# Hybrid encoder with PEER experts: one store for two blocks' GELU values, and transfers moved from ScalarE to SyncE

## The reference

```python
q = (xc @ w_q).reshape(c, PEER_HEADS, 2, PEER_HALF_DIM)
sc = jnp.einsum('chpd,hpnd->chpn', q, sub_keys)
top_s, top_i = lax.top_k(sc, kk)                  # 16 of 128 per half
...
cand_s, cand_i = lax.top_k(cand.reshape(c, PEER_HEADS, kk * kk), kk)
experts = i1 * PEER_N_KEYS + i2                   # 16 of 16384 per head
gates = jax.nn.softmax(cand_s, axis=-1)
act = gelu(einsum('chkd,cd->chk', u[experts], xc))
out = einsum('chk,chkd->cd', gates * act, v[experts])
```

## Time and profile before

| | us |
|---|---|
| runs shown (3): median, lowest, highest | 3271.24, 3267.51, 3274.54 |
| the profiled execution: its time, its span | 3269.31, 3267.5 |
| TensorE busy (share of the span) | 3141.4 (96%) |
| VectorE, GpSimd, ScalarE busy | 2429.8, 1987.1, 1451.7 |
| mean granted TensorE clock | 0.987 of 2.4 GHz |
| ScalarE waiting for the `gelu_d` store, both layers | 177.6 in 76 waits |

### The profile page before, as it was taken

One profiled execution on the slowest core, in us unless ns is written; L12 is line 12 of the kernel. 1 busy time (PEld: TensorE's weight loads), 2 busy tenths in 40 slices (PEclk: granted clock), 3 DMA queues, 4 the chain that ended last, 5 costly groups with the idle time before them and its releaser, 6 DMA issues. The chain is left out here.

```text
span 3267.5 us, 61700 instructions
## 1 busy us (share of the span) xinstructions
PE 3141.4 (96%) x18584; PEld 2847.5 (87%) x18584; DVE 2429.8 (74%) x5191; ACT 1451.7 (44%) x2596; POOL 1987.1 (61%) x1588
## 2 busy tenths in 40 slices
PE   8998999999899999999899999999998989999997
PEld 8878889999898888888798787999998988888886
DVE  1475548888776799999915746488887867999998
ACT  2464234444676533333324633444446764333332
POOL 3454348888664566666545543588886645666665
PEclk9999999999999999999999999999999999999999
DMA  4002139999797799999820021499998967999996
GB/s 166 32 2 78 53 111 325 328 325 329 260 349 259 260 336 336 336 334 331 278 90 24 2 85 58 143 321 322 325 307 266 347 246 278 335 335 335 335 331 224
DMA packets 255581, 779.16 MB, mean 238 GB/s; under 512 B 30176, under 2 KB 97504, under 8 KB 247520
## 3 DMA queue, kind: packets, MB, share of 16 engines
q1 hardware_dynamic: 170400, 455.75, 41.9%
q0 software_dynamic: 78336, 285.25, 23.5%
q10 hardware_dynamic: 6720, 36.74, 2.9%
HBM read 692.66 MB, written 83.89 MB: 238 GB/s over the span
## 5 line engine op out<-in xcount | busy, mean ns | idle before, releaser
L723 POOL TENSOR_TENSOR st_lo<-st_raw,st_hi 128x1024 fp32r<-128x1024 f32 x290 | 697.5, 2405 | 416.2 <-ACT st_hi L1003 410.4
L1003 ACT CAST st_hi<-st_raw 128x1024 fp32r<-128x1024 f32 x544 | 569.9, 1048 | 659.1 <-PE ps L2194 615.9
L2091 PE MATMUL ps<-t_hi,st_hi 128*128 128x368 f32 (+1 forms) x2288 | 780.8, 341 | 0.8 <-ACT st_hi L1003 0.7
L2092 PE MATMUL ps<-t_lo,st_hi 128*128 128x368 f32 (+1 forms) x2288 | 770.5, 337 | 0.0
L837 POOL TENSOR_TENSOR wt_lo<-w_f,wt_hi 128x384 fp32r<-128x384 f32 x256 | 416.3, 1626 | 317.6 <-ACT wt_hi L1167 317.5
L2095 PE MATMUL ps<-t_hi,st_lo 128*128 128x368 f32 (+1 forms) x2288 | 448.1, 337 | 3.6 <-POOL st_lo L723 3.5
L2091 PEld LDWEIGHTS ps<-t_hi,st_hi 128*128 128x128 f32 x2288 | 430.3, 188 | 13.3 <-ACT st_hi L1003 3.0
L2092 PEld LDWEIGHTS ps<-t_lo,st_hi 128*128 128x128 f32 x2288 | 430.8, 188 | 10.1
L2095 PEld LDWEIGHTS ps<-t_hi,st_lo 128*128 128x128 f32 x2288 | 394.6, 188 | 17.2 <-POOL st_lo L723 6.2
L2194 PE MATMUL ps<-st_hi,wt_hi 128*128 128x512 f32 x1536 | 390.0, 389 | 2.7 <-ACT wt_hi L1167 2.7
L2194 PE MATMUL ps<-st_lo,wt_hi 128*128 128x512 f32 x1536 | 389.7, 389 | 0.0
(11 more groups left out here) (236 smaller groups left out, 5141.9 us busy)
## 6 DMA issues: line engine op xcount, KB each, us to landing
st_raw<-in_peer_u SPq DMA_DIRECT2D x256, 512.0 KB
st_raw<-in_peer_v SPq DMA_DIRECT2D x256, 512.0 KB
gelu_d<-h_out SPq DMA_DIRECT2D x256, 184.0 KB
h_in<-gelu_d SPq DMA_DIRECT2D x256, 184.0 KB
gates_d<-g_stage ACTq DMA_DIRECT2D x32, 1024.0 KB
g_ch<-gates_d SPq DMA_DIRECT2D x56, 512.0 KB, 6.0
w_raw<-in_w_in SPq DMA_DIRECT2D x16, 1168.0 KB, 5.2
st_raw<-in_peer_w_q SPq DMA_DIRECT2D x32, 512.0 KB
```

The source lines that it names most:

```text
L723: nc.gpsimd.tensor_tensor(st_lo[:, s].rearrange("p c f -> p (c f)"), st_raw[:, r], st_hi[:, s].rearrange("p c f -> p (c f)").bitcast(F32), ...
L1003: nc.scalar.copy(st_hi[:, r % 2].rearrange("p c f -> p (c f)"), st_raw[:, r]).then_inc(st_h, 1)
L2091: nc.tensor.matmul(dst, st_hi[:, s, c], t_hi[:, c, rows], start=c == 0, stop=False)
L2092: nc.tensor.matmul(dst, st_hi[:, s, c], t_lo[:, c, rows], start=False, stop=False)
```

## The change

`h_out` gets four buffers in two pairs, `gelu_d` is laid out by pairs, and a store moves the two blocks of a pair (`gelu_store(i, q)` waits for both GELUs). ScalarE's GELU of a pair waits for the store of the pair two before. The transfers of `idx`, `x_x`, `h_x` and the gate stores are no longer issued by ScalarE; SyncE issues them, between its loads, in an order that is written out from block 88 on. Some small tiles (`idx_x`, `e_x`, `h_x`, `idx_u`, `idx_b`, `dot_8`) move to where `wt_hi` and `wt_lo` of the v half lie. TensorE's, VectorE's and GpSimd's instructions are the same, in the same order.

```diff
-    h_out = pr.tile("h_out", [P, 2, TN], F32)
+    h_out = pr.tile("h_out", [P, 2, 2, TU], F32)
...
-    gelu_d = nc.dram_tensor("gelu_d", [EB, P, TU], F32, kind="Internal").ap()
+    gelu_d = nc.dram_tensor("gelu_d", [EB // 2, P, 2, TU], F32, kind="Internal").ap()
...
-            def gelu_store(i, s):
+            def gelu_store(i, q):
-                sp.wait_ge(gelu_done, EB * l + 2 * i + s + 1 + PRIME)
-                sp.dma_start(gelu_d[2 * i + s], h_out[:, s, 0:TU]).then_inc(s_hst[s], 16)
+                sp.wait_ge(gelu_done, EB * l + 2 * i + 2 + PRIME)
+                sp.dma_start(gelu_d[i], h_out[:, q]).then_inc(s_hst[q], 16)
...
-                sp.dma_start(h_in[:, s, 0:TU], gelu_d[2 * i + s]).then_inc(s_gh[s], 16)
+                sp.dma_start(h_in[:, s, 0:TU], gelu_d[i][:, s]).then_inc(s_gh[s], 16)
...
-            with sp.Fori(0, EB // RAW - 2) as i:
+            def u_quad(i, r):
+                if r % 2:
+                    gelu_store(2 * i + r // 2, r // 2)
+                st_load(2 * i + QB // 2 + RAW // 2 + 1 + r // 2, (r + 2) % RAW, a["peer_u"][l, RAW * i + RAW + 2 + r])
+
+            def gates_store(body, part):
+                w, q = divmod(body, BODIES)
+                if 0 < w < WIN - 1:
+                    n_q = NK // STORES
+                    n0 = q * 2 * n_q + part * n_q
+                    sp.wait_ge(g_ev, TN // GRP * l + WIN_T // GRP * w + RING)
+                    sp.dma_start(gates_d[:, w - 1, ds(n0, n_q)],
+                                 g_stage[:, (w - 1) % 2, ds(n0, n_q)]).then_inc(s_gst[(w - 1) % 2], 16)
+
+            n_pre = 2 * PRE // RAW
+            per = XG // RAW
+            with sp.Fori(0, n_pre) as i:
                 for r in range(RAW):
-                    gelu_store(2 * i + r // 2, r % 2)
-                    st_load(2 * i + QB // 2 + RAW // 2 + 1 + r // 2, (r + 2) % RAW, a["peer_u"][l, RAW * i + RAW + 2 + r])
+                    u_quad(i, r)
+            for r in range(RAW):
+                u_quad(n_pre, r)
+                sp.wait_ge(x_numbers, l + 1)
+                for g in range(per * r, per * (r + 1)):
+                    sp.dma_start(idx[g * XT:(g + 1) * XT, SLOTS:DOTS],
+                                 idx_x[P - XT:P, g * XR:(g + 1) * XR]).then_inc(s_xn, 16)
+            for r in range(RAW):
+                u_quad(n_pre + 1, r)
+                for g in range(per * r, per * (r + 1)):
+                    sp.dma_start(x_x[g * XT:(g + 1) * XT], x_tok[P - XT:P, TB - 1]).then_inc(s_xx, 16)
+            for body in range(2, B_ROUNDS):
+                for r in range(RAW):
+                    if r < 2:
+                        gates_store(body, r)
+                    u_quad(n_pre + body, r)
             for b in range(EB - 2 * RAW, EB - 2):
-                gelu_store(b // 2, b % 2)
+                gates_store(B_ROUNDS + (b - EB + 2 * RAW) // 2, b % 2)
+                if b == 2 * PRE + RAW * B_ROUNDS + 2:
+                    sp.wait_ge(x_gelu, l + 1)
+                    for g in range(XG):
+                        sp.dma_start(h_x[P - XT:P, g * XR:(g + 1) * XR],
+                                     dots[g * XT:(g + 1) * XT, SLOTS:DOTS]).then_inc(s_xh, 16)
+                if b % 2:
+                    gelu_store(b // 2, b // 2 % 2)
...
-            def gelu(m, s):
+            def gelu(m, s, half, q):
...
-                act.wait_ge(s_hst[s], (EB // 2 * l + m + 1) * 16)
-                nc.scalar.activation(h_out[:, s, 0:TU], ps[:, s, 0:TU], ACT.Gelu).then_inc(gelu_done, 1)
+                act.wait_ge(s_hst[q], (EB // 4 * l + half + 1) * 16)
+                nc.scalar.activation(h_out[:, q, s], ps[:, s, 0:TU], ACT.Gelu).then_inc(gelu_done, 1)
```

More of the change, by code:

```diff
@@ L296, in build @@
     sp_r = Region(shared + VALUE_BYTES)
+    w_sp_at = sp_r.end
     idx_f = sp_r.tile("idx_f", [P, SLOTS], F32)
     idx = sp_r.tile("idx", [P, DOTS], U32)
[L299 to L302, removed]
     idx_v = sp_r.tile("idx_v", [P, 2, VRING], U32)
-    idx_b = sp_r.tile("idx_b", [P, 2, BDOTS], U32)
     e_sp = sp_r.tile("e_sp", [P, SLOTS], F32)
-    dot_8 = sp_r.tile("dot_8", [P, URING], F32)
     dots = sp_r.tile("dots", [P, DOTS], F32)
-    w_sp = sp_r.tile("w_sp", [P, SLOTS], F32)
+    w_sp = nc.alloc_sbuf_tensor_at("w_sp", [P, SLOTS], F32, offset=w_sp_at)
     gb = Region(shared)
@@ L323, in build @@
     w_f = vp.tile("w_f", [P, 2, TN], F32)
-    x_x = nc.alloc_sbuf_tensor_at("x_x", [P, D], F32, offset=vp.end)
-    assert vp.end >= tk.end and D <= 4 * TN
+    xr = Region(vp.end)
+    x_x = xr.tile("x_x", [P, D], F32)
+    idx_x = xr.tile("idx_x", [P, SLOTS], U32)
+    e_x = xr.tile("e_x", [P, SLOTS], F32)
+    h_x = xr.tile("h_x", [P, SLOTS], F32)
+    idx_u = xr.tile("idx_u", [P, 2, URING], U32)
+    idx_b = xr.tile("idx_b", [P, 2, BDOTS], U32)
+    dot_8 = xr.tile("dot_8", [P, URING], F32)
+    assert vp.end >= tk.end
     wt_hi = vp.tile("wt_hi", [P, 2, TN], F32R)
     wt_lo = vp.tile("wt_lo", [P, 2, TN], F32R)
+    assert xr.end <= vp.end
     ga = Region((limit - 2 * NK * WIN_T * 4) // 64 * 64)
@@ L503, in _ @@
                 gated_load(0, s)
-            for s in range(2):
-                gelu_store(EB // 2 - 1, s)
+            gelu_store(EB // 2 - 1, (EB // 2 - 1) % 2)
             sp.wait_ge(st_used, ST_PER * l + QB + EB + PRIME)
@@ L1077, in _ @@
                 nc.scalar.copy(g_t[:] if k == 2 else i_t[:, k], ps[:, SEL_BANKS[k], 0:TN]).then_inc(sel_act, 1)
-            act.wait_ge(x_numbers, l + 1)
-            for g in range(XG):
-                act.dma_start(idx[g * XT:(g + 1) * XT, SLOTS:DOTS],
-                              idx_x[P - XT:P, g * XR:(g + 1) * XR]).then_inc(s_xn, 16)
-            for g in range(XG):
-                act.dma_start(x_x[g * XT:(g + 1) * XT], x_tok[P - XT:P, TB - 1]).then_inc(s_xx, 16)
             def gate_group(body, g, share):
@@ L1103, in keep_gates, with stage_body @@
                 nc.scalar.copy(g_stage[:, sw, :, ds(q * BODY_T + GRP * g, GRP)], parts_of(g)).then_inc(g_ev, 1)
-            def stage_body(w, sw, q, store, pairs, share, after):
+            def stage_body(w, sw, q, pairs, share, after):
                 body = w * BODIES + q
                 load_table(body + PRE + 1)
-                if store:
-                    n_q = NK // STORES
-                    act.wait_ge(g_ev, TN // GRP * l + WIN_T // GRP * w + RING)
-                    for part in range(2):
-                        n0 = q * 2 * n_q + part * n_q
-                        act.dma_start(gates_d[:, w - 1, ds(n0, n_q)],
-                                      g_stage[:, 1 - sw, ds(n0, n_q)]).then_inc(s_gst[1 - sw], 16)
                 act.wait_ge(s_gst[sw], (STORES * (WIN_D * l + (w - sw) // 2) + 1) * 16)
@@ L1149, in _ @@
                             nc.scalar.activation(dots[:, SLOTS:DOTS], dots[:, SLOTS:DOTS], ACT.Gelu).then_inc(x_gelu, 1)
-                            act.wait_ge(x_gelu, l + 1)
-                            for g in range(XG):
-                                act.dma_start(h_x[P - XT:P, g * XR:(g + 1) * XR],
-                                              dots[g * XT:(g + 1) * XT, SLOTS:DOTS]).then_inc(s_xh, 16)
             for g in range(GROUPS):
```

17 lines of the change are left out of this document (9 added, 8 removed).

## The result

The changed kernel took 3219.3 us in the median of 4 executions (3217.34 to 3234.61) against 3269.38 before: ratio 0.9854, 95% interval 0.9825 to 0.9884. The profiled execution took 3217.34 us, span 3215.5; the one of before 3269.31, span 3267.5. The forecast was 3240.5 with a range from 3228 to 3256: the sign was right, the size was not, and the time lies under the range.

The account below looks back on a forecast made before the run. TensorE, busy 96% of the span, was taken as the bound, stopped by ScalarE issuing transfers. Gains 6.6 + 7.3 + 7.6 + 7.3 + 1 = 29.8 us from 3269.3 gave 3239.5; forecast median 3240.5, range 3228 to 3256.

Parts of the forecast that it names:

- The holes: TensorE's two waits per layer in the gates, 7.4 to 7.6 us each; shortening them was forecast to give 28.8 us.
- The first hole: TensorE's wait for `oh`: idx and x_x issues leave ScalarE, gaining 6.6 us in layer 0, 7.3 in layer 1.
- The second: TensorE's wait for the `g_stage` copy: h_x issues and gate stores leave ScalarE, gaining 7.6 and 7.3 us.
- the clock: TensorE's clock in the waits that remain: no fall taken; bounds were nothing or 2.7 us in each layer.
- rival 1: First hole stays cold: clock falls in the remaining 3.5 and 2.3 us, 5.4 us less gain, 3247; chance 0.17.
- layer 0's loop: Expert loop of layer 0: paired stores and four buffers gain 1 us, taken from 0 to 13.
- layer 1's: Expert loop of layer 1: TensorE does not wait there and runs at an unexplained slower pace, so nothing gained.
- My bound of 13: Upper bound on layer 0's loop loss: 86 blocks at 4.09 us each against 3.93, up to 13 us.
- GpSimd the blame for late `st_lo`: Layer 0's loop: GpSimd, busy 18 of 20 us, holds `st_lo` up by itself, so 1 us of 0 to 13.
- Rival 3: A loop's pace changes with placement of code or buffers: 15 us either way, 3225 or 3256; chance 0.07.
- Rival 2: Layer 0's loop runs undisturbed as ScalarE no longer waits for stores: 9 us more, 3231.5; chance 0.12.

Follow-up runs that it names:

- e4: The changed kernel run again, unchanged: median 3233.89 us, ratio 0.9869 against the kernel before.
- e10: The changed kernel run a third time, unchanged: median 3223.27 us, ratio 0.9853 against the kernel before.
- e15: The changed kernel run a fourth time, unchanged: median 3233.87 us, ratio 0.9859 against the kernel before.
- e2: Against the changed kernel, all moved issues go back to ScalarE; paired stores and four buffers stay: median 3263.49 us, ratio 0.9961 against the kernel before.
- e5: Against the changed kernel, one store for each block instead of one for two, four buffers kept: median 3235.35 us, ratio 0.9868 against the kernel before.
- e1: The kernel before, unchanged, profiled a second time: median 3276.34 us, ratio 1.0005.
- e3: Against the changed kernel, one store a block from two buffers; moved issues stay on SyncE: median 3247.67 us, ratio 0.9914 against the kernel before.
- e6: Against the kernel before, only the idx and x_x issues moved to SyncE, small tiles at their new places: median 3262.5 us, ratio 0.9962.
- e7: Against the kernel before, only the 8 h_x issues a layer moved to SyncE, small tiles at their new places: median 3263.61 us, ratio 0.9965.
- e11: Against the kernel before, only the gate stores moved to SyncE, small tiles at their new places: median 3271.76 us, ratio 0.9999.

## Why the prediction was right and wrong

**The holes: right.** 29.5 us measured in the gates against 28.8. A part of this closeness is luck: over the four profiles of the kernel after and the two of the kernel before, the gates differ by 27.5 us on average, mainly because in two of the four layer 0's blocks there took 5.94 us, not 5.76. The first hole kept 2.2 us in either layer where I had 3.5 and 2.3: in layer 0 the gathered row came sooner against TensorE's stop than before. The second kept 1.10 where I had 1.4 (7.58 less 6.2); it now ends with VectorE's `oh`.

For the clock I took no fall, and that held in one layer only. It stayed at 1.00 behind the first hole of layer 0, and fell to 0.72 on average behind that of layer 1 (shown above). Of the eight first holes in the four profiles of the kernel after (after, e4, e10, e15), all of 2.2 to 2.3 us, two had such a fall behind them. The other is in layer 1 of e4:

```profile
2440.00:2450.00 10.00, 7.68 (x42) 7.52 (x41) 8.58 (x18) 5.74 (x17) 8.53 (x6) 0.83 0.90 317
```

From the first `st_lo` matmul of the block ahead of the hole to that of the block behind it, layer 1 took 9.82 and 9.90 us in the two with a fall, 8.18 and 8.23 in e10 and e15. So rival 1 comes with one execution and not with the next, at some 1.7 us, and the measured profile paid it once. Alone, the moves gave 28.1 us in the medians.

**The term that failed: layer 0's loop at 1 us of 0 to 13, layer 1's at nothing.** Layer 0's loop gave 8.3 us. The stalls alone were worth 9.8, by e2 and e5, which ran it at 3.97 us a block in 525.4 and 525.5; the kernel after ran it at 4.00 and lost 1.5 again. Layer 1's loop gave 16.5, in this profile all by the pace; when the kernel before runs it at 3.97, as in e1, the stores cost some 9.5 there too (535.1 against 525.6). Two readings were at fault. First, I took TensorE's wait for `st_lo` from its matmuls. The stall stands in the row of the weight loads, which need `st_lo` and `st_hi` first (they run ahead of the matmuls in flight, as the Trainium skill has it: TensorE: Matmul & The Clock Gate, Architectural detail). Weight loads of the kernel before, 467 to 820, busy us and mean, then idle:

```profile
L2091 PEld LDWEIGHTS ps<-t_hi,st_hi 128*128 128x128 f32 x693 | 129.8, 187 | 3.3 <-ACT st_hi L1003 3.0 <-issue 0.2
L2095 PEld LDWEIGHTS ps<-t_hi,st_lo 128*128 128x128 f32 x688 | 115.3, 188 | 6.5 <-POOL st_lo L723 6.2
```

That is 9.8 us, where the matmuls' rows of the same stretch show 0.8 and 3.6: a matmul is drawn 0.33 us long while one starts every 0.166, so its end covers a part of each gap. After the change both rows read 0.0. My bound of 13 had the right size: it took 3.93 us a block from 122 records in 20 us, a count that includes matmuls cut by the stretch's ends. The order of time of the kernel before shows 3.97,

```profile
517.05 1.48 PE L2095 MATMUL ps<-t_hi,st_lo 128*128 128x368 f32 x8
...
521.02 1.49 PE L2095 MATMUL ps<-t_hi,st_lo 128*128 128x368 f32 x8
```

and 351.4 less 86 x 3.97 is 10.0. Second, I gave GpSimd the blame for late `st_lo`, and so took 1 of the 13. The chain began at ScalarE: the GELU waits for a store, the cast stands behind it, `st_lo` behind that. In e5 no GELU waits for a store, GpSimd is as busy as before (282 us from 500 to 818, 276 in the kernel before), and both rows read 0.0: it keeps up.

**The pace: a rival that I priced and set aside.** Rival 3 had 15 us either way at 0.07; it was 16.5 in this profile. Rival 2 had 9 us at 0.12; it was 8.3. I treated them as alternatives to the forecast and to each other, and the range took in the whole of rival 2 but only half of rival 3. They don't exclude each other, and both came. The forecast, less what layer 0's loop, layer 1's and the gates gave beyond it, and with the 1.4 and 0.9 lost elsewhere: 3239.5 - 7.3 - 16.5 - 0.7 + 2.3 = 3217.3, the profiled time. A pace that I saw at two values in one profile, and could not explain, was owed its 15 us in the range with every other case, not a rival of its own.

What the change is worth without that luck: its 18 executions on four chips have a mean of 3231.1 us, 78 executions of the kernel before 3274.6: 43.5 us, and between 41 and 47 in each of the four places where both ran. With e3's 28.1 for the moves that leaves some 15 for the buffers, near e2's 12.3. The forecast of 29.8 missed that second part.

## What to carry to other kernels

Read a TensorE stall in the weight loads' row as well as in the matmuls', and against the period of the blocks; 3.6 us in the matmuls' row were 9.8 on the clock. A wait that a profile doesn't show in one layer may be hidden by something else in that one execution, here a slower pace: where two layers run the same code, take the price from the layer that shows it, and profile the kernel before twice. Move small issues off an engine that another one waits for in short stages; they were worth something only in the two places where TensorE stood still (e6: 16 issues, 9.8 us of ScalarE's time, gave 6.1 and 6.5 us a layer; e7: 8 issues, 5.0 us, gave 6.5 and 6.0, the clock's part included), while the 16 gate stores alone gave nothing (e11).

## What the chip showed that was not expected

The same 24 matmuls take 3.97, 4.00 or 4.16 us at a granted clock of 1.00, one matmul of 368 columns 0.1655, 0.1667 or 0.1733 us. The value holds to 0.01 us a block for up to 88 blocks, until TensorE stands still, even for 1.1 us, and may then be another. Of the 16 loops profiled with four buffers and no added pause, eight took 525 to 528 us and eight 542. Executions of one kernel so lie 16 us apart for each loop.

The gates stages have two paces as well. A block with two groups, 24 + 16 matmuls, takes 5.76 us in the profile of after and 5.94 in e4's, 32 blocks a layer, nearly 6 us; this, and not the holes, is why the gates of layer 0 took 262.0 and 261.2 us in e4 and e15 against 255.4 in after and e10. Block starts in layer 0, first after, then e4:

```profile
941.35 1.48 PE L2119 MATMUL ps<-t_hi,st_lo 128*128 128x368 f32 x8
...
947.11 1.48 PE L2119 MATMUL ps<-t_hi,st_lo 128*128 128x368 f32 x8
```

```profile
942.99 1.55 PE L2119 MATMUL ps<-t_hi,st_lo 128*128 128x368 f32 x8
...
948.93 1.55 PE L2119 MATMUL ps<-t_hi,st_lo 128*128 128x368 f32 x8
```

The sums over V, with 512 columns, know no second pace: they start every 0.227 us in all 18 profiles.

The Trainium skill (TensorE: Matmul & The Clock Gate, Back-to-back issue gap) has one value for a matmul by itself at full clock, columns by 2.4 GHz and about 2.5 ns, 155.8 ns for 368 columns, and says that weight loads between the matmuls change the spacing; the spacings of the 368 columns here lie 10 to 18 ns above, at three values for one stream, and the measurement decides. What sets the pace stays open: neither chip, nor kernel, nor the number of stalls does by itself, and no run here changed the weight loads or the order of the matmuls, or what other engines and transfers read and write meanwhile, on purpose to see it.
